# Turning seven heads' outputs by transposing DMAs in a two-layer trunk: a change of engine for 28 turns

## What is computed

```python
proj = x @ w_in                                # (1024, 3*2048 + 16)
xm, z, o_pre = the three blocks of 2048 columns
xc = silu(causal_conv(xm))                     # 4 taps, per channel
q, k, v = per head: xch @ w_q, xch @ w_k, xmh @ w_v      # 8 heads, DK 128, DV 256
h = _mlstm_chunkwise(q, k, v, i_pre, log_sigmoid(f_pre)) # 8 chunks of 128 positions
hn = (h - mean(h)) * rsqrt(var(h) + eps) * norm_g        # over the 256 values of a head
hb = sigmoid(o_pre) * hn + skip * xc
branch = (hb * silu(z)) @ w_out
x = layer_norm(alpha * x + branch)
```

## Time and profile before

| what | value |
|---|---|
| time, three runs | 1389.78, 1390.51, 1393.87 us |
| span of the profiled execution | 1388.6 us |
| PE busy | 1377.9 us, 99% |
| DVE busy | 1156.8 us, 83% |
| ACT busy | 755.9 us, 54% |
| POOL busy | 150.8 us, 11% |
| PE's mean granted clock | 0.999 of full |

### The profile page before, as it was taken

One profiled execution on the slowest core, in us unless ns is written; L12 is line 12 of the kernel. 1 busy time (PEld: TensorE's weight loads), 2 busy tenths in 40 slices (PEclk: granted clock), 3 DMA queues, 4 the chain that ended last, 5 costly groups with the idle time before them and its releaser, 6 DMA issues.

```text
span 1388.6 us, 19102 instructions
## 1 busy us (share of the span) xinstructions
PE 1377.9 (99%) x6602; PEld 1155.1 (83%) x6602; DVE 1156.8 (83%) x1892; ACT 755.9 (54%) x1321; POOL 150.8 (11%) x250
## 2 busy tenths in 40 slices
PE   9999999999999999999999999999999999999997
PEld 7888888888888888888888888888888888888886
DVE  7889989898989989899874456797888888889976
ACT  6775766748576675757743436564333333436340
POOL 2002011010101111010000001001111111100021
PEclk9999999999999999999999999999999999999999
DMA  6115344362433526345497667434666656689661
GB/s 231 52 40 144 93 109 128 76 173 63 136 100 92 144 61 171 78 138 175 135 335 241 222 196 219 127 122 117 166 152 169 157 139 155 178 284 338 216 198 76
DMA packets 103744, 213.43 MB, mean 154 GB/s; under 512 B 10962, under 2 KB 27858, under 8 KB 102498
## 3 DMA queue, kind: packets, MB, share of 16 engines
q1 hardware_dynamic: 90850, 178.66, 38.7%
q0 software_dynamic: 12800, 33.56, 12.9%
HBM read 170.11 MB, written 75.63 MB: 177 GB/s over the span
## 4 chain that ended last, share of the span: by engine, by line
PE 98%; DVE 1%; DMA 0%; ACT 0%; POOL 0%; issue 0%; DVEq 0%; SPq 0%; POOLq 0%; ACTq 0%
PE wide L2954 21%; PE wide L2956 21%; PE wide L2955 21%; PE ps_state L2954 3%; PE ps_state L2956 3%; PE ps_state L2955 3%; PE ps_inter L2955 2%; PE ps_inter L2954 2%; PE ps_inter L2956 2%; PE ps_intra L3134 2%; PE ps_intra L2954 2%; PE ps_s L2954 2%; PE ps_intra L2956 2%; PE ps_s L2955 2%; PE ps_s L2956 2%; PE ps_intra L2955 2%
## 5 line engine op out<-in xcount | busy, mean ns | idle before, releaser
L2955 PE MATMUL wide<-xa,inb 128*128 128x512 f32 x576 | 224.7, 390 | 0.0
L2954 PE MATMUL wide<-xb,inb 128*128 128x512 f32 x472 | 189.6, 402 | 0.4 <-DVE z_buf L1993 0.4
L2956 PE MATMUL wide<-xb,inb 128*128 128x512 f32 x472 | 184.4, 391 | 0.0
L2955 PEld LDWEIGHTS wide<-xa,inb 128*128 128x128 f32 x576 | 108.4, 188 | 20.3
L2955 PE MATMUL wide<-xa,blk 128*128 128x512 f32 x320 | 124.5, 389 | 0.0
L2956 PEld LDWEIGHTS wide<-xb,inb 128*128 128x128 f32 x472 | 88.6, 188 | 19.2
L2954 PEld LDWEIGHTS wide<-xb,inb 128*128 128x128 f32 x472 | 88.8, 188 | 18.3 <-issue 1.3
L2954 PE MATMUL wide<-xb,blk 128*128 128x512 f32 x256 | 99.7, 389 | 0.0
L2956 PE MATMUL wide<-xb,blk 128*128 128x512 f32 x256 | 99.6, 389 | 0.0
L1875 ACT ACTIVATE wy<-wy_raw 128x1024 fp32r<-128x1024 f32 x56 | 59.4, 1062 | 60.6 <-DMA wy_raw<-y_block 60.5
L2954 PE MATMUL wide<-xa,inb 128*128 128x512 f32 x208 | 83.2, 400 | 0.6 <-DVE inb L1956 0.6
(11 more groups left out here) (454 smaller groups left out, 3966.3 us busy)
## 6 DMA issues: line engine op xcount, KB each, us to landing
in_raw<-in_w_in SPq DMA_DIRECT2D x45, 512.0 KB, 4.2
wy_raw<-y_block SPq DMA_DIRECT2D x56, 256.0 KB, 4.5
mw_raw<-h_block SPq DMA_DIRECT2D x53, 256.0 KB, 3.6
m_sum<-in_w_out POOLq DMA_DIRECT2D x48, 256.0 KB, 4.2
h_block<-f_buf SPq DMA_DIRECT2D x48, 256.0 KB, 2.7
w_sum<-in_pool_w_out POOLq DMA_DIRECT2D x48, 256.0 KB, 4.4
a_raw<-in_pool_w_z SPq DMA_DIRECT2D x16, 512.0 KB, 3.9
a_raw<-folded SPq DMA_DIRECT2D x16, 512.0 KB, 4.4
```

Source lines behind the costliest of these rows:

```text
L2954: pe.matmul(dst, a[0], b[0], start=first, stop=False, skip_group_check=more)
L2955: pe.matmul(dst, a[0], b[1], start=False, stop=False, skip_group_check=more)
L2956: return pe.matmul(dst, a[1], b[0], start=False, stop=last, skip_group_check=more)
```

## The change

For heads 0 to 6 the PE transposes are left out. In their place, for each half f of a head:

- `part_turn` (ACT, two operations of 128x1024): reads the normalised four chunks as 16-bit numbers and writes their low halves and their high halves apart, into `apart`.
- `move_turned` (SP): waits for `part_turn`, then issues two transposing DMAs of 128x1024 16-bit numbers (256 KB each), from `apart` to `turned_halves`, both in SBUF.
- `join_turn` (ACT, two operations of 128x1024): waits for both DMAs and puts the halves together again as 32-bit numbers in `joined`.
- `y_turned` (DVE) reads `joined` in place of the PSUM bank.

`apart` and `joined` lie over `xm_hi` (the bytes that `qT` and `kT` use later), `turned_halves` over `num`. So `part_turn` also waits until the head's last scores are made, and `high_xm(h)` until `joined` was read. On ACT `high_qkv` goes from the first half to the second, and on DVE the statistics and scales of f = 1 come earlier and `y_turned` and `y_finish` later. Three semaphores are shared with later stages to make room for the new ones.

```diff
+            def move_turned(h, f):
+
+                sp.wait_ge(h_apart, 2 * h + f + 1)
+                for part in range(2):
+                    sp.dma_start_transpose(turned_at(f, part), apart[:, f, part, :]).then_inc(h_moved, 16)
...
             for h in range(1, HEADS):
                 load_in(3 * h + 1, 0)
                 load_in(3 * h + 1, 1)
+                move_turned(h - 1, 0)
                 load_qkv(h)
                 load_in(3 * h + 2, 0)
                 load_rows(h)
+                move_turned(h - 1, 1)
                 store_h(h - 1, 1, 2)
                 load_in(3 * h + 2, 1)
...
             def high_xm(h, n):
                 act.wait_ge(conv_ready, 2 * h + 2)
-                if h == 0:
+                if h:
+                    act.wait_ge(turn_taken, 4 * h)
+                else:
...
+            def part_turn(h, f, part):
+
+                act.wait_ge(hn_ready, 2 * h + f + 1)
+                act.wait_ge(s_full, NC * (h + 1))
+                ins = act.activation(apart[:, f, part, :].rearrange("p (c d) -> p c d", d=DV),
+                                     num[:, 4 * f:4 * f + 4, 0:DV].bitcast(U16).rearrange("p c (d b) -> p c d b", b=2)[:, :, :, part], ACT.Copy)
+                if part:
+                    ins.then_inc(h_apart, 1)
+
+            def join_turn(h, f, part):
+
+                act.wait_ge(h_moved, 64 * h + 32 * (f + 1))
+                ins = act.activation(joined[:, f, :, :].bitcast(U16).rearrange("p j (c t b) -> p c j t b", t=P, b=2)[:, :, :, :, part],
+                                     turned_at(f, part).rearrange("p (c j) t -> p c j t", j=2), ACT.Copy)
+                if part:
+                    ins.then_inc(turn_full, 2)
...
-                turned = (ps_inter, ps_s)[m % 2][:, :] if b is None else b
+                turned = joined[:, n, j, :] if b is None else b
...
-                if h:
-                    if (kind, q) == (X_OF, 5):
-                        turn_head(h - 1, 0)
-                    elif (kind, q) == (Z_OF, 1):
-                        turn_head(h - 1, 1)
-                    elif (kind, q) == (Z_OF, 6):
-                        turn_head(h - 1, 2)
-                    elif (kind, q) == (Z_OF, 7):
-                        turn_head(h - 1, 3)
```

More of the change, by code:

```diff
@@ L32 @@
 F32R = mybir.dt.float32r
+U16 = mybir.dt.uint16
 P = 128
@@ L325, in build @@
                 xc_hi = sA("xc_hi", [P, 2, S], F32R, whole)
+            with ExitStack() as whole:
+                turned_halves = sA("turned_halves", [P, 2 * NC * (DV + 1)], U16, whole)
             num = sA("num", [P, NC, DV + 1])
@@ L332, in build @@
                 xm_hi = sA("xm_hi", [P, 2, S], F32R, whole)
+            with ExitStack() as whole:
+                apart = sA("apart", [P, 2, 2, S], U16, whole)
+            with ExitStack() as whole:
+                joined = sA("joined", [P, 2, 2, HALF], F32, whole)
             qT = sA("qT", [P, S])
@@ L462, in in_loaded, with turned_at @@
             return (w_first_in[j], 16) if p == 1 else (w_half_in[j], 16 * max(p, 1))
+        def turned_at(f, part):
+            at = f * (2 * S + PAD) + part * S
+            return turned_halves[:, at:at + S].rearrange("p (n t) -> p n t", t=P)
         def by_chunk(row):
@@ L579, in build @@
         hn_ready = sem("hn_ready")
+        h_apart = sem("h_apart")
+        h_moved = sem("h_moved")
         turn_full = sem("turn_full")
@@ L602, in build @@
         fold_taken = sem("fold_taken")
-        x0_hi = sem("x0_hi")
+        x0_hi, X0_HI = h_apart, 2 * (HEADS - 1)
         x0_lo = sem("x0_lo")
@@ L633, in build @@
         ln_done_late = sem("ln_done_late")
-        wg_in = sem("wg_in")
+        wg_in, WG_IN = h_moved, 64 * (HEADS - 1)
         wu_in = [sem(f"wu_in{r}") for r in range(WU_RING)]
@@ L1448, in first_half @@
                 take_num(h - 1, 6)
+                part_turn(h - 1, 0, 0)
+                part_turn(h - 1, 0, 1)
                 take_num(h - 1, 7)
@@ L1451, in first_half @@
                 in_high(x + 11)
+                join_turn(h - 1, 0, 0)
+                join_turn(h - 1, 0, 1)
+                in_snapshot(3 * h + 1, 1)
                 in_high(x + 12)
-                in_snapshot(3 * h + 1, 1)
+                norm_head(h - 1, 1)
+                part_turn(h - 1, 1, 0)
+                part_turn(h - 1, 1, 1)
                 first_tap(h, 1)
                 in_high(x + 13)
-                high_qkv(h)
-                norm_head(h - 1, 1)
                 in_high(x + 14)
@@ L1465, in second_half @@
                 in_upper_right(3 * h)
+                join_turn(h - 1, 1, 0)
+                join_turn(h - 1, 1, 1)
                 in_snapshot(3 * h + 1, 5)
@@ L1468, in second_half @@
                 in_high(x + 17)
+                high_qkv(h)
                 in_high(x + 18)
@@ L2261, in first_half @@
                 in_sum(3 * h + 1, 0)
-                y_turned(h - 1, 0)
+                chunk_stats(h - 1, 6)
                 in_sum(3 * h + 1, 1)
-                y_turned(h - 1, 1)
+                chunk_stats(h - 1, 7)
+                scales(h - 1, 1)
                 in_low(x + 10)
-                chunk_stats(h - 1, 6)
                 in_sum(3 * h + 1, 2)
+                norm_scale(h - 1, 1)
                 in_sum(3 * h + 1, 3)
                 in_join(3 * h, 4)
-                chunk_stats(h - 1, 7)
-                scales(h - 1, 1)
+                y_turned(h - 1, 0)
                 in_low(x + 11)
+                y_turned(h - 1, 1)
                 in_join(3 * h + 1, 2)
+                in_low(x + 12)
                 y_finish(h - 1, 0)
-                norm_scale(h - 1, 1)
+                y_finish(h - 1, 1)
                 tap(h, 1, 1)
-                in_low(x + 12)
-                y_finish(h - 1, 1)
                 in_low(x + 13)
@@ L2281, in first_half @@
                 in_low(x + 15)
-                y_turned(h - 1, 2)
-                y_finish(h - 1, 2)
             def second_half(h):
@@ L2288, in second_half @@
                 tap(h, 1, 2)
+                y_turned(h - 1, 2)
                 tap(h, 1, 3)
+                y_finish(h - 1, 2)
+                y_turned(h - 1, 3)
                 in_sum(3 * h + 2, 0)
-                y_turned(h - 1, 3)
                 in_join(3 * h + 1, 5)
@@ L2572, in first_half_lo @@
             def first_half_lo(n):
-                dve.wait_ge(x0_hi, n + 1)
+                dve.wait_ge(x0_hi, X0_HI + n + 1)
                 at = (B11, B21)[n // 4]
@@ L3151, in turn @@
                 mm.then_inc(turn_full, 1)
-            def turn_head(h, m):
-                if m == 1:
-                    pe.wait_ge(s_taken, NC * (h + 1))
-                elif m:
-                    pe.wait_ge(turn_taken, 4 * h + m - 1)
-                turn(h, m, (ps_inter, ps_s)[m % 2])
             pe.wait_ge(const_set, 2)
```

2 lines of the change are left out of this document (1 added, 1 removed).

## The result

The changed kernel takes 1425.83 us (median of 4 runs, 1425.5 to 1427.62); the kernel before took 1392.19 beside it (4 runs, 1389.78 to 1395.64). The ratio is 1.0248, 95% interval 1.0235 to 1.0261: 2.5% slower, 34 us, where 9 were forecast. The spans of the two profiled executions differ by 37.2 us (1425.8 against 1388.6).

A forecast was written before the change was run, and what follows sets the result against it. PE was taken to bound the kernel, with DVE close behind. 12.5 us gained on PE against over 21 lost to waits for DVE made it 9.1 us slower, 1400 us; likeliest 1394 to 1411, range 1381 to 1440.

The forecast's parts named there:

- The worth of the turns: On PE, 28 turns of 0.45 us left out save 12.5 us; DVE as second bound lets less through.
- rival A: Short trip between SBUF places, D = 2.5 us: each head gains 1.2 us, 1382 us in all; chance 0.27.
- The chain to the third `y_turned`: Serial steps through ACT, SP and DMAs, two trips and four ACT pairs of 2.0 us, ending at 370.1 + 2D.
- T: Start of the third `y_turned` on DVE in the walked head, forecast at 379.5 us.
- D: Round trip from `part_turn`'s end until both transposing DMAs land, twice a head: 4.7 us, likeliest 4.35 to 5.5.
- The tap's wait for `first_tap`: On DVE, the tap waits 1.7 us for ACT's `first_tap`, now behind `norm_head` and `part_turn`.
- POOL's mask: POOL's 1.24 us operation at 373.06 was to meet the tap on DVE, which then ends near 375.8.
- From T to product 94: From the third `y_turned` along DVE to PE's start of the head's product 94: 12.65 us.
- The forecast wait of PE for the low part of product 94: PE idle ahead of products 89 and 94, waiting for `in_low` on DVE, some 3 us a head.
- One head walked through, times seven: Heads 0 to 6 taken as alike, so one head's 1.3 us loss makes 9.1 us.
- 14 us for each us of D: D counts twice in each of seven heads, so each us of D adds 14 us to the total.
- rival C: Slow transposing DMAs, D = 6.2 us: T = 382.5, a head costs 4.3 us, 1420 us in all; chance 0.27.

The follow-up runs named there:

- e3_tiny: Changed kernel without DMAs, the four ACT operations of a half shrunk to next to nothing, heads not turned: 1382.7 us, 0.994 of the kernel before.
- e2_no_trip: Changed kernel without the transposing DMAs, all eight ACT operations of a head kept, the join reading `num`: 1391.47 us, 1.0005 of the kernel before.
- e12_bank_late: Changed kernel with one DVE operation, `in_join` of product 91's bank, moved ahead of `y_finish`, the fourth `y_turned` and `in_sum`: 1419.06 us.
- e1_copy: Changed kernel with plain DMAs of the same bytes in place of the transposing ones, halves not turned: 1406.15 us, 1.0113 of the kernel before.
- e9_overlap: Changed kernel reordered: `norm_head` and `part_turn` of f = 1 ahead of the first join so both trips overlap, taps ahead of `y_turned`: 1430.02 us.
- e5_bank: Changed kernel with the bank's eviction on ACT ahead of the second join and its `in_join` on DVE ahead of the third `y_turned`: 1433.73 us.
- e11_overlap: As e9_overlap, but SP issues the O pair's second load ahead of the stores that wait for `y_finish`: 1417.13 us.

## Why the prediction was right and wrong

**The worth of the turns**: right in size. Of PE's 12.5 us DVE lets 8.4 through by the prediction, and e3_tiny measured 7.8. What is wrong is that a short trip with all the ACT operations would leave this gain (rival A): with no trip at all e2_no_trip took 1391.5, not 1382. The prediction had DVE at the third `y_turned` at 377.0, held by nothing; in e2_no_trip it starts at 377.59, behind the join, and PE still waits 10.9 us for the bank.

**The chain to the third `y_turned`**: right in its steps, 1.9 us short in this head. T was forecast at 379.5 and is 400.57 - 19.15 = 381.4. Of this D is 0.6: the trips were 4.54 and 5.47 us, against 2 x 4.7. The joins are 0.9: a pair takes 2.45 from start to next start, not 2.0, since one writes every second 16-bit number and takes 1.35 us, while `part_turn`, which reads so, took the 1.05 assumed. The rest, 0.4, are wake-ups and overlaps. The tap's wait for `first_tap` was forecast at 1.7 and is 1.68:

```profile
393.70 1.28 DVE L2058 SCALAR_TENSOR_TENSOR xx<-xx,cols 128x1024 f32<-128x1024 f32 x1 [1.68 <-ACT xx L1292]
...
395.63 2.19 DVE L2005 TENSOR_TENSOR inb<-in_raw,inb 128x512 fp32r<-128x512 f32 x2
```

POOL's mask, at 396.11 here, did not meet this tap but the two low parts behind it (2.19 us for two, where two steps of 0.6 are 1.2).

**From T to product 94**: here the prediction failed. It had 12.65 and it was 14.43, because it followed DVE alone, from `in_sum` to the end of the low part, and asked for PE only at the end. Between the two stands `in_join`, for which PE waited 0.4 us once in all heads before, and which is now 3.6 us late for product 91. From product 91 on it is PE that counts: 4.56 us to its start and 8.2 for 36 matmuls at the full clock would have been 12.8, hardly more than forecast, and the lower clock behind the wait adds the 1.6. So the bank's wait in itself is worth next to nothing in this head; the clock that falls behind it is what costs. The forecast wait of PE for the low part of product 94 is in no head. With `in_join` two microseconds earlier (e12_bank_late) the same stretch is 12.72, and this wait is there. The prediction's last sentence named a wait for a bank as the mark of a missed place, and that is what it was.

**The sum**: a head was to cost 1.3 us; this one cost 5.0, of which 1.9 are the chain's and 1.8 this step's. The head was also no fair sample: heads cost 2.8 to 8.4 us. Neither the trips nor the clock were the same in all of them. "One head walked through, times seven" held for neither. As an estimate over seven heads, by the prediction's own rule of 14 us for each us of D: 9.1 forecast, some 10 for trips of 5.4 in the mean and not 4.7, 9 for the joins and overlaps (1.3 a head), and 9 for the lower clock are 37, where the table ends at 37.5. D's mean lies inside the 4.35 to 5.5 of the forecast case, 1394 to 1411, so that case was missed by the other terms: the joins, and the bank with the clock, for which it had no term. That 1425.8 lies in the wide range of 1381 to 1440 is luck: the range was drawn for trips up to 7.6 us.

**What D decides**: "14 us for each us of D" fits between trips of 4 and 5.4 us. From the changed kernel to the plain copies the mean from `part_turn` to join falls from 5.4 to 4.1 us, which by the rule is 18 us; measured are 20. It doesn't reach down to nothing: at the second trip ACT has 3.6 us of other operations ahead of the join (e2_no_trip), so that a shorter one wins nothing there. In e1_copy the second join waits for its DMAs in two heads only. Between e2_no_trip and the changed kernel, with 5.4 at the mean, are 34 us.

**SP**: I took 0.4 us for an issue, and a transposing one holds SP for 1.24 to 1.32, 2.62 for the pair. The Trainium skill's page DMA: Bandwidth & Descriptors, section Why a DMA increments its semaphore by 16 and not by 1, from which I had estimated 1.5 to 1.7 and set aside, was nearer than my row. The 1309 ns a block of the Trainium skill's page VectorE: DVE Perf Modes, section The three transpose paths, do not add up one after another here: the eight 128x128 blocks of a DMA landed in 3.7 us. In this head SP's longer hold still did not make D the 6.2 of rival C: the first trip is the hold of the first DMA and the landing of the second, 1.28 and 3.21 in the chain above. In heads 0, 2 and 5 the first trip was 6.4 to 7.3, by a later landing and not by a longer hold (in head 2 the second DMA lands 5.91 us behind its issue). Rival C's time of 1420 was passed with a mean D of 5.4, and its low part of product 87, held past PE, is there in four heads; the rest came by the joins, the bank and the clock.

**What stays open**: why the lower clock comes in some heads of one execution and not in others with a wait of like length; why three of the first trips landed 2 to 3 us later; whether the trips cost anything where nobody waits for them; whether an order exists in which a half by DMA wins.

## What to carry to other kernels

When work moves from the bounding engine to a serial chain, walk not only the chain to its end but every operation that is queued behind its last wait, and ask for each who waits for it: here `in_join`, five places behind the third `y_turned`, held a PSUM bank. A wait of PE of 2 to 4 us can cost more than its length: in the changed kernel the matmuls behind six of eight such waits ran at half the clock, and that came back to the engine that caused it. A walk through one head is a sample of one: look at the spread of its waits over the others. Before reordering one queue look at what waits at the head of the others: a store ahead of a load on SP cost 13 us (e9_overlap), and an ACT operation that waits for PE ahead of one on the chain cost more than the reordering brought (e5_bank).

## What the hardware showed that I had not expected

- A transposing DMA of 128x1024 16-bit numbers from SBUF to SBUF holds SP for 1.24 us at the least (median 1.32), the plain one of the same bytes for 0.47 (0.55); they land in 3.7 and 2.6 us (medians).
- ACT takes 1.05 us to read every second 16-bit number of a row and write them packed, and 1.35 us to read packed and write every second one (128x1024 each). Where it reads every second one too (e2_no_trip) it takes 1.36, so the writing sets it.
- The granted clock was 0.51 for 3.5 us after 3.6 us without a matmul, and stayed at 1.00 after waits of 1.34 and 0.97. The length of the wait alone does not tell: it was 0.52 behind a wait of 2.00 us in head 1 of the changed kernel and 1.00 behind one of 2.02 in head 6, and 1.00 behind one of 3.16 in head 0 of e11_overlap.
